# A two-block transformer kernel on Trainium2: other instruction orders in four feed-forward layers and in the head of the latent attention

## The reference, cut to what matters

```python
# first_block, D_MODEL 1024, SEQ 512, DEPTH 2, D_FF 2816
sc = silu(c)
for i in range(2):
    mod = (sc @ ada_w[i] + ada_b[i]).reshape(B, 9, 1024)        # shifts, scales, gates
    x = modulated_sublayer(x, mod[:, 0:3], ..., swiglu)          # ffn0, then ffn2
    x = modulated_sublayer(x, mod[:, 3:6], ..., pool_mixer if i == 0 else mla_mixer)
    x = modulated_sublayer(x, mod[:, 6:9], ..., swiglu)          # ffn1, then ffn3
# swiglu: (silu(gate) * up) @ w_out, gate and up = split(h @ w_in)
# mla_mixer, 16 heads:
lat = h @ w_in; c_q, c_kv, k_r = split(lat, [256, 384])
c_q = rmsnorm(c_q, q_norm); c_kv = rmsnorm(c_kv, kv_norm)
q = einsum(c_q, w_uq); q_rope = apply_rope(q[..., 64:], cos, sin) * ATTN_SCALE
k_rope = apply_rope(k_r, cos, sin); q_lat = einsum(q[..., :64], w_uk) * ATTN_SCALE
p = softmax(q_lat . c_kv + q_rope . k_rope); o = ((p . c_kv) . w_uv) @ w_o
# second_block: two hybrid layers of stick-breaking and sparse attention (the change does not touch them)
```

## Time and profile before

| | us |
|---|---|
| median of 3 runs | 2932.2 |
| lowest and highest | 2930.58, 2932.82 |
| the profiled execution | 2932.32 |
| its span | 2930.5 |
| TensorE busy | 2805.9 |
| mean granted clock of TensorE | 0.984 |

### The profile page before, as it was taken

How to read it: one execution, slowest core, us unless ns; L and a number is a source line. 1 busy time by engine, 2 the same in 40 slices (tenths; PEclk the granted TensorE clock), 3 DMA queues, 4 the chain that set the end, 5 groups by cost and what they waited for, 6 DMA issues and landing times. The chain is left out here.

```text
span 2930.5 us, 42964 instructions
## 1 busy us (share of the span) xinstructions
PE 2805.9 (96%) x16774; PEld 2451.4 (84%) x16774; DVE 2185.0 (75%) x3427; ACT 1448.7 (49%) x2390; POOL 401.0 (14%) x297
## 2 busy tenths in 40 slices
PE   8999989999999999799999999999899999999999
PEld 7998778998889988677799988787788778877887
DVE  7888778888778877899687755387677663866773
ACT  6555235555255542566465632464555435555552
POOL 0010111000101001100300000404300233141003
PEclk9999999999999999999999999999999999999999
DMA  7675733665636656200245432402211232022113
GB/s 271 194 224 172 238 126 76 207 203 174 233 115 214 208 168 215 73 12 19 101 119 162 145 107 87 136 15 83 91 52 58 96 127 72 30 94 72 54 56 115
DMA packets 103065, 367.40 MB, mean 125 GB/s; under 512 B 11984, under 2 KB 14800, under 8 KB 102352
## 3 DMA queue, kind: packets, MB, share of 16 engines
q1 hardware_dynamic: 73968, 262.95, 25.8%
q0 software_dynamic: 26304, 90.19, 11.7%
q10 hardware_dynamic: 2592, 11.51, 1.1%
HBM read 354.12 MB, written 6.29 MB: 123 GB/s over the span
## 5 line engine op out<-in xcount | busy, mean ns | idle before, releaser
L464 ACT ACTIVATE w_hi<-raw 128x1024 fp32r<-128x1024 f32 x351 | 366.8, 1053 | 320.1 <-DMA raw<-stream_in 179.1
L485 POOL TENSOR_TENSOR w_lo<-raw,w_hi 128x1024 fp32r<-128x1024 f32 x109 | 274.2, 2522 | 1265.1 <-ACT w_hi L464 1265.0
L506 PE MATMUL psum<-h_hi,w_hi 128*128 128x256 f32 (+1 forms) x1609 | 352.3, 329 | 8.5 <-DVE h_lo L699 3.4
L506 PE MATMUL psum<-h_lo,w_hi 128*128 128x256 f32 (+1 forms) x1609 | 345.4, 325 | 0.0
L506 PE MATMUL psum<-h_hi,w_lo 128*128 128x256 f32 (+1 forms) x1609 | 345.2, 325 | 0.0
L479 DVE TENSOR_TENSOR w_lo<-raw,w_hi 128x1024 fp32r<-128x1024 f32 x202 | 247.2, 1227 | 83.1 <-ACT w_hi L464 82.9
L506 PE MATMUL psum<-t_hi,w_hi 128*128 128x256 f32 (+1 forms) x1536 | 284.9, 300 | 19.9 <-ACT sq L1156 7.5
L464 ACT ACTIVATE w_hi<-xr 128x1024 fp32r<-128x1024 f32 x202 | 213.5, 1057 | 160.6 <-DVE xr L1271 68.6
L506 PEld LDWEIGHTS psum<-h_hi,w_hi 128*128 128x128 f32 x1609 | 251.0, 188 | 44.1 <-DVE w_lo L479 5.8
L506 PE MATMUL psum<-t_hi,w_lo 128*128 128x256 f32 (+1 forms) x1536 | 283.3, 299 | 0.0
L506 PEld LDWEIGHTS psum<-h_lo,w_hi 128*128 128x128 f32 x1609 | 252.0, 188 | 26.9
(11 more groups left out here) (527 smaller groups left out, 5568.4 us busy)
## 6 DMA issues: line engine op xcount, KB each, us to landing
raw<-stream_in SPq DMA_DIRECT2D x351, 512.0 KB, 3.4
ada_raw<-ada_in POOLq DMA_DIRECT2D x128, 512.0 KB, 5.3
xr<-stream_in SPq DMA_DIRECT2D x122, 512.0 KB, 4.6
xr<-stream_in POOLq DMA_DIRECT2D x40, 512.0 KB, 5.5
ada_in_t<-ada_in SPq DMA_DIRECT2D x8, 512.0 KB, 12.0
x_held<-X ACTq DMA_DIRECT2D x2, 2048.0 KB, 6.8
X<-x_held ACTq DMA_DIRECT2D x2, 2048.0 KB, 7.9
X<-xT_in SPq DMA_DIRECT2D x4, 512.0 KB, 5.5
```

The costliest lines, as they stand in the source:

```text
L464: act.activation(w_hi[:, u % RING], tile, ACT.Copy, scale=-1.0 if u in negated else 1.0).then_inc(hi_ready, 1)
L485: pool.tensor_tensor(w_lo[:, u % RING], source[u][0], w_hi[:, u % RING].bitcast(F32), ALU.subtract).then_inc(lo_ready, 1)
L506: mm = pe.matmul(dst, w[wi], m[mi], start=(first and n == 0), stop=(last and n == total - 1), skip_group_check=skip)
```

## The change

In the feed-forward layers a table `PAIR_ROWS` gives each pair its own number of rows. ffn0 gets 22 rows in its pairs (two in pairs 1 and 2, three in pairs 3 to 8; the third stands behind the second weight sum of the next pair) and 26 in its down stage; ffn1 and ffn2 keep two rows in each of pairs 1 to 8 and get another order of their 24 rows in the down stage, with none behind the second unit. GpSimd's queue issues as many transfers per pair as the pair has rows, still ahead of the accumulating transfer. In pair 0 of all four layers the copy of the third product stands ahead of the sixth unit's high half and of the high half of a sum.

In the latent attention ScalarE copies and scales the rotary banks (before, VectorE did), VectorE multiplies by the cosine straight from PSUM into `lat`, the low halves of the first query unit, the keys and the values are made by VectorE, and those of the rotary unit and from the second query unit on by GpSimd as before. ScalarE makes the second query unit's high half after the four rotary high halves.

```diff
@@ -290,7 +290,7 @@
         snap = Signal(sem("products_kept"))
         joined = Signal(sem("products_joined"))
         parts_negated, odd_added = sem("parts_negated"), sem("odd_added")
-        t2_copied = sem("t2_copied")
+        t2_copied, rotary_copied = sem("t2_copied"), sem("rotary_copied")
         a_hi_ready = Signal(sem("a_hi_ready"))
         a_ready = Signal(sem("a_ready"))
 
@@ -1005,10 +1005,11 @@
 
         ADA = {"ffn0": range(2, 8), "ffn1": range(8, 13), "ffn2": range(13, 18), "ffn3": ()}
         SHIFT_BY_PE = (1, 2, 4, 6)
-        FIRST_PAIR = {"ffn0": 1, "ffn1": 1, "ffn2": 1}
+        PAIR_ROWS = {"ffn0": (0, 2, 2, 3, 3, 3, 3, 3, 3, 0), "ffn1": (0,) + 8 * (2,) + (0,),
+                     "ffn2": (0,) + 8 * (2,) + (0,)}
         FIRST_ROWS = {"ffn0": 0, "ffn1": 0, "ffn2": 0}
-        DOWN_ROWS = {"ffn0": (0, 1, 1, 2, 2, 1, 2, 2, 1, 2, 2, 1, 2, 2, 1, 2, 2, 1, 2, 2, 1, 0, 0, 0),
-                     "ffn1": (0, 1, 1, 1, 1, 1, 1, 2, 1, 1, 2, 1, 1, 2, 1, 1, 1, 2, 1, 1, 1, 0, 0, 0)}
+        DOWN_ROWS = {"ffn0": (0, 0, 1, 2, 1, 1, 2, 1, 1, 2, 1, 1, 2, 1, 1, 2, 1, 1, 2, 2, 1, 0, 0, 0),
+                     "ffn1": (0, 0, 1, 1, 2, 1, 1, 2, 1, 1, 2, 1, 1, 2, 1, 1, 2, 1, 1, 1, 1, 0, 0, 0)}
         DOWN_ROWS["ffn2"] = DOWN_ROWS["ffn1"]
 
 
@@ -1019,13 +1020,13 @@
 
         def ada_pair_dve(dve, L, j, m):
 
-            if ADA[L] and FIRST_PAIR[L] <= j < PAIRS - 1:
-                ada_blocks_dve(dve, L, FIRST_ROWS[L] + 2 * (j - FIRST_PAIR[L]) + m, 1)
+            if ADA[L] and m < PAIR_ROWS[L][j]:
+                ada_blocks_dve(dve, L, FIRST_ROWS[L] + sum(PAIR_ROWS[L][:j]) + m, 1)
 
         def ada_down_dve(dve, L, k):
 
             if ADA[L]:
-                ada_blocks_dve(dve, L, FIRST_ROWS[L] + 2 * (PAIRS - 1 - FIRST_PAIR[L]) + sum(DOWN_ROWS[L][:k]), DOWN_ROWS[L][k])
+                ada_blocks_dve(dve, L, FIRST_ROWS[L] + sum(PAIR_ROWS[L]) + sum(DOWN_ROWS[L][:k]), DOWN_ROWS[L][k])
 
         def pair_banks(j):
 
@@ -1186,12 +1187,15 @@
             if final:
                 a_hi_act(act, L, 0)
             keep_act(act, L, j, "p5", 1, "v2")
+            if j == 0:
+                keep_act(act, L, j, "u2", 2, "g2")
             split_hi(act, u + 5)
             if final:
                 a_hi_act(act, L, 1)
             if j == 0:
                 combine_hi_act(act, L, T4)
-            keep_act(act, L, j, "u2", 2, "g2")
+            else:
+                keep_act(act, L, j, "u2", 2, "g2")
             split_hi(act, u + 6)
             if final:
                 a_hi_act(act, L, 2)
@@ -1323,6 +1327,7 @@
                 a_lo_dve(dve, L, 3)
             split_lo(dve, u + 8)
             sum_2_dve(dve, L, j + 1)
+            ada_pair_dve(dve, L, j, 2)
             up_sum_dve(dve, L, j)
             if final:
                 a_lo_dve(dve, L, 4)
@@ -1433,10 +1438,9 @@
                     ada_piece(pool, t)
                     t += 1
             for j in range(PAIRS):
-                if ADA[L] and FIRST_PAIR[L] <= j < PAIRS - 1:
+                for _ in range(PAIR_ROWS[L][j] if ADA[L] else 0):
                     ada_piece(pool, t)
-                    ada_piece(pool, t + 1)
-                    t += 2
+                    t += 1
                 add_weights(pool, L, j + 1)
             if ADA[L]:
                 for t in range(t, min((ADA[L][-1] + 1) * NC + 2, 18 * NC)):
@@ -2004,7 +2008,7 @@
                 prod.give(mm, ("u", u) if c == 3 else ("g", g + c))
             first_products = mla_extra(L)
             for r in range(4):
-                pe.wait_ge(evac.sem, evac.at(("g", g + r)))
+                pe.wait_ge(rotary_copied, r + 1)
                 if r:
                     pe.wait_ge(scaled.sem, scaled.at((L, "rot", r - 2 if r >= 2 else "k")))
                 sums.give(pe.matmul(psum[:, ROTARY_BANKS[r % 2]], mconst[:], rotary(r), start=True, stop=True),
@@ -2065,17 +2069,29 @@
             for c in range(2):
                 split_value_act(act, (L, "cq", c), ta[:, c], cq_hi[:, c])
             split_value_act(act, (L, "kv"), tb[:, 0], kv_hi[:])
+            u, g = u + 4, g + 4
+
+            def copy_rotary(r):
+
+                act.wait_ge(prod.sem, prod.at(("g", g + r)))
+                act.activation(rotary(r), bank(g + r), ACT.Copy, scale=ATTN_SCALE).then_inc(rotary_copied, 1)
+            split_hi(act, u + 1)
+            act.wait_ge(h_ready.sem, h_ready.at((L, "cq", 1)))
+            copy_rotary(0)
+            split_hi(act, u + 2)
+            copy_rotary(1)
             act.wait_ge(scaled.sem, scaled.at((L, "rot", "k")))
             for rows, first in ((slice(64, 96), 0), (slice(32, 64), 1)):
                 op = act.activation(kt_hi[rows, first:4:2], tb[rows, 1:2].broadcast_to((32, 2, S)), ACT.Copy)
             part_hi.give(op, (L, "rot", "k"))
-            u, g = u + 4, g + 4
-            for k in range(1, 5):
-                split_hi(act, u + k)
+            copy_rotary(2)
+            copy_rotary(3)
+            split_hi(act, u + 3)
             for r in range(4):
                 if r == 2:
                     mla_extra(L)(act, "act", -1)
-                split_value_act(act, (L, "rot", r), tb[:, r % 2], qr_hi[:, r])
+                split_value_act(act, (L, "rot", r), lat[:, r], qr_hi[:, r])
+            split_hi(act, u + 4)
             softmax_act(act, L, mla_attention, mla_extra(L))
             u, g = own[L, "wo"], own[L, "wog"]
             split_hi(act, u + 1)
@@ -2119,36 +2135,43 @@
             split_value_dve(dve, (L, "kv"), tb[:, 0], kv_hi[:], kv_lo[:])
             dve.wait_ge(stage_loaded, own[L, "loaded"])
             rotate_dve(dve, order, (L, "rot", "k"), lat[:, 3], mrope[:, 0], mrope[:, 1], psum[:, 4], tb[:, 1])
+            u, g = u + 4, g + 4
+
+            def by_cosine(r):
+                dve.wait_ge(rotary_copied, r + 1)
+                evac.give(dve.scalar_tensor_tensor(out=lat[:, r], in0=bank(g + r), scalar=ATTN_SCALE, in1=mrope[:, 0],
+                                                   op0=ALU.mult, op1=ALU.mult), ("g", g + r))
+
+            def by_sine(r):
+                dve.wait_ge(sums.sem, sums.at((L, "rot", r)))
+                order.step(dve.tensor_tensor((std, rstd)[r % 2][:], psum[:, ROTARY_BANKS[r % 2]], mrope[:, 1],
+                                             ALU.mult))
+                dve.wait_ge(evac.sem, evac.at(("g", g + r)))
+                scaled.give(dve.tensor_tensor(lat[:, r], lat[:, r], (std, rstd)[r % 2][:], ALU.add),
+                            (L, "rot", r))
+            dve.wait_ge(lo_ready, u + 1)
+            split_lo(dve, u + 1, early=True)
+            by_cosine(0)
+            by_cosine(1)
+            split_lo(dve, u + 2, early=True)
+            by_cosine(2)
+            by_cosine(3)
+            by_sine(0)
+            by_sine(1)
             dve.wait_ge(part_hi.sem, part_hi.at((L, "rot", "k")))
             for rows, first in ((slice(64, 96), 0), (slice(32, 64), 1)):
                 op = dve.tensor_tensor(kt_lo[rows, first:4:2], tb[rows, 1:2].broadcast_to((32, 2, S)),
                                        kt_hi[rows, first:4:2].bitcast(F32), ALU.subtract)
             h_ready.give(op, (L, "rot", "k"))
-            u, g = u + 4, g + 4
-            for r in range(4):
-                dve.wait_ge(prod.sem, prod.at(("g", g + r)))
-                evac.give(dve.tensor_scalar(rotary(r), bank(g + r), ATTN_SCALE, None, ALU.mult), ("g", g + r))
-            def by_cosine(r):
-                dve.wait_ge(evac.sem, evac.at(("g", g + r)))
-                dve.wait_ge(h_ready.sem, h_ready.at((L, "rot", r - 2 if r >= 2 else "k")))
-                order.link(dve.tensor_tensor(tb[:, r % 2], rotary(r), mrope[:, 0], ALU.mult))
-
-            def by_sine(r):
-                dve.wait_ge(sums.sem, sums.at((L, "rot", r)))
-                order.step(dve.tensor_tensor((std, rstd)[r % 2][:], psum[:, ROTARY_BANKS[r % 2]], mrope[:, 1],
-                                             ALU.mult))
-                scaled.give(dve.tensor_tensor(tb[:, r % 2], tb[:, r % 2], (std, rstd)[r % 2][:], ALU.add),
-                            (L, "rot", r))
-            for first in (0, 2):
-                by_cosine(first)
-                by_cosine(first + 1)
-                by_sine(first)
-                by_sine(first + 1)
-                if first == 2:
-                    dve.wait_ge(part_hi.sem, part_hi.at((L, "zeros")))
-                    mla_extra(L)(dve, "dve", -1)
-                for r in (first, first + 1):
-                    split_value_dve(dve, (L, "rot", r), tb[:, r % 2], qr_hi[:, r], qr_lo[:, r])
+            split_lo(dve, u + 3, early=True)
+            for r in (0, 1):
+                split_value_dve(dve, (L, "rot", r), lat[:, r], qr_hi[:, r], qr_lo[:, r])
+            dve.wait_ge(part_hi.sem, part_hi.at((L, "zeros")))
+            mla_extra(L)(dve, "dve", -1)
+            by_sine(2)
+            by_sine(3)
+            for r in (2, 3):
```

(4 more changed lines are left out.)

## The result

The changed kernel takes 2947.4 us in the median of four runs (2946.1 to 2948.3), the kernel before in four runs beside it 2931.4: the ratio is 1.0054, with a 95% interval from 1.0039 to 1.0070. It is slower by half a per cent, and the interval leaves out 1. The prediction said 2949.4 us, slower. The changed kernel's profiled execution has a span of 2944.9 us, 14.4 more than that of before.

The account below looks back on a forecast made before the run. TensorE was taken to bound the kernel, busy 96% of the span, with VectorE ending the pairs. Terms 27.7 - 5.6 - 3.6 - 0.8 - 3.6 + 3.0 = +17.1 us on 2932.3 gave 2949.4 us, range 2937 to 2958.

Parts of the forecast that it names:

- the row that leaves the second unit: Down stages of three layers: one row (1.22 us) moves from ahead of the last activation low half; -1.2 us each.
- first layer, pairs: Pairs 3 to 8: third row delays the accumulating transfer on GpSimd's queue, period 24.5 us over 19.89; +27.7 us (18.1 to 31.9).
- first layer, down stage: 26 rows instead of 32 end three TensorE waits for weights, -5.6 us; one row leaving the second unit, -1.2 us.
- second layer: One row leaves the down stage's second unit, -1.2 us; earlier copy of the third product in the first pair, -0.8 us.
- third layer: One row leaves the down stage's second unit, -1.2 us; the first pair's earlier copy gains zero.
- latent attention: Head of the attention: scores start later because the rotary rows' transfers wait on SyncE's queue; +3.0 us.
- last layer: First pair, no rows: earlier third-product copy ends TensorE's 1.9 us wait and the half clock's 1.7; -3.6 us.
- the bound above: First layer's pairs: upper bound of 7.6 us for the accumulating transfer's landing, from the third of three transfers.
- Rival 4: First layer's six pairs: half clock after TensorE's waits makes it last in the pair, 10.2 us more, 2959.6 us; chance 0.08.
- SyncE's wait: Attention's head: rotary transfers issue only after a fetch whose buffer GpSimd's second-query-unit low half frees; scores 3.0 us later.
- First pairs: Pair 0, four layers: earlier third-product copy ends TensorE's 1.9 us wait; kept 0.8 us in second, 3.6 in last layer.
- Rival 1: Pairs and attention: neither queue holds anything, pairs cost 7.3 us and the attention wins 5.2; 2920.8 us, chance 0.08.

Follow-up runs that it names:

- the rows alone: Kernel before with only the first layer's row changes: its tables, the third row in pairs 3 to 8 and `ffn_pool`; 2952.4 us, ratio 1.0069.
- the old rows: Changed kernel with the first layer's rows as before the change (two in pairs 1 to 8, 32 in its down stage); 2931.8 us, ratio 0.9991.
- the order of two transfers: Changed kernel with the accumulating transfer issued ahead of the third row's transfer in the six three-row pairs; 2924.1 us, ratio 0.9971.
- the version with both moves: Changed kernel, accumulating transfer ahead of the third row's and second query unit's high half ahead of the rotary high halves; 2916.7 us, ratio 0.9952.
- the kernel with the high half moved: Changed kernel with ScalarE making the second query unit's high half before the four rotary high halves; 2939.6 us, ratio 1.0023.

## Why the prediction was right, and where a size was off

Set side by side, instruction by instruction of TensorE, the two first profiles give each step's share (the rows "first layer, down stage", "second layer" and "third layer" hold the prediction's -1.2 us for the row that leaves the second unit):

| step | predicted us | measured us |
|---|---|---|
| first layer, pairs | +27.7 | +31.9 |
| first layer, down stage | -6.8 | -9.3 |
| second layer | -2.0 | -2.0 |
| third layer | -1.2 | -1.3 |
| latent attention | +3.0 | +4.2 |
| last layer | -3.6 | -3.7 |
| what no step covers, first block | 0 | -2.1 |
| second block | 0 | -3.3 |
| sum | +17.1 | +14.4 |

The total is nearer than its terms, and that is luck: pairs and attention cost 5.4 us more than forecast, and the down stage and the two lines without a step took 7.9 back. Those two lines are scatter as far as the runs show it: 3.3 us of the second block (above), and most of the 2.1 is TensorE at a clock of 0.50 at the ends of the second layer and of the attention, for 10.3 and 3.4 us in the first profile of before, for 6.9 us and not at all in that of the changed kernel; over all thirteen profiles the first stretch lasts 3.4 to 10.3 us and the second up to 6.9.

**Pairs.** The mechanism is shown by three runs: the rows alone bring the loss, the old rows undo most of it, and the order of two transfers takes back all but VectorE's 1.22 us a row. The size was 4 us short. The period was 25.0 to 25.5 us instead of 24.5, for the landing that no row of before showed took 7.4 us, not the 6.9 that I took from the second of three transfers; 7.6, the bound above, was closer; and VectorE's stretch took 14.61 us in the pair shown, not 14.40. Issued without a row's transfer right ahead, the same transfer landed in 5.9. The Trainium skill (DMA: Bandwidth & Descriptors, Anatomy of one DMA) would have 3.2 us, as an estimate, for either; both rows disagree.

**Rival 4, the clock**, was right about half of it. TensorE fell to half clock at each of the six waits, yet VectorE's mark at the end of the pairs moved by 32.0 us (254.58 to 286.53), as TensorE's did: the half clock lay under VectorE's loop, which the prediction gave as the reason against it.

**Down stage.** The three waits went as said; some 2.5 us more went with them, 1.0 of it a wait for ScalarE at the layer's end, which the prediction didn't have. The row that leaves the second unit did what was forecast: TensorE's wait there falls from 1.49 to 0.34 us in the first and second layer and from 1.49 to 0.33 in the third. Only the traces show it; no run takes it by itself.

**Attention.** SyncE's wait was there, and moving one instruction removes it. Of the 1.2 us that were missing, the landing of the fourth rotary transfer took 2.5 us instead of 2.0, and the last rotary sum ended 0.4 us later than worked out. GpSimd's start was named rightly. What the prediction left out is TensorE's 4.84 us wait for the low half of the values' unit. It lies inside the longer chain and cost at most those 0.4 us: the last rotary products come behind it, and VectorE's order of time has a short pause for them:

```profile
1254.96 0.69 DVE L2147 TENSOR_TENSOR rstd<-psum,mrope 128x512 f32<-128x512 f32 x1 [0.29 <-PE psum L2014]
```

**First pairs.** Three layers keep 0.8 us or less of TensorE's 1.9 us and the last keeps it all, as predicted; the half clock behind it follows in some executions and not in others, so its 1.7 us are a chance, not a constant.

**Rival 1** is the version with both moves: neither queue holds anything. It was priced at 2920.8 us, 0.9961 of the kernel before, and measured at 0.9952. That is near in part by luck: the attention won 3.2 us (23.8 instead of 27.0 from the first query product to the scores), not 5.2, since GpSimd's low half now runs beside VectorE's two rotary lows and makes them some 2.1 us longer; the down stage's further 2.5 us made up for it.

## What to carry to other kernels

Where an engine issues transfers in order, a transfer added for one purpose holds whatever is queued behind it until its own wait is over: read the queue's order before you count the new work, and put the transfer that someone waits for ahead of the one that must wait. When a step is moved, follow what it frees (here a buffer, then a fetch, then the transfers behind that fetch), for the wait turns up two engines away. And removing a wait pays only up to the next one in the chain: moving the low half of the values' unit, and the copies in three layers, gave TensorE its time back, and it waited nearly as long later on.

## What the runs showed of the hardware that was not expected

**A GpSimd instruction beside VectorE.** An instruction of VectorE with two operands in SBUF took three times as long while GpSimd's low half ran, and ended just after it. Orders of time of GpSimd and of VectorE, the version with the low half of the values' unit moved:

```profile
1219.84 2.56 POOL L485 TENSOR_TENSOR w_lo<-raw,w_hi 128x1024 fp32r<-128x1024 f32 x1 [13.21 <-ACT w_hi L464]
```

```profile
1220.10 0.68 DVE L2151 TENSOR_TENSOR rstd<-psum,mrope 128x512 f32<-128x512 f32 x1
1220.82 2.13 DVE L2154 TENSOR_TENSOR lat<-lat,rstd 128x512 f32<-128x512 f32 x1
1222.97 2.44 DVE L2168 TENSOR_TENSOR kt_lo<-tb,kt_hi 32x1024 fp32r<-32x1024 f32 x2
```

The first of VectorE's rows reads PSUM and one SBUF operand and takes its usual 0.68 us; the second has two in SBUF and takes 2.13 instead of 0.69, ending 0.55 us after GpSimd's (1222.40); the key low halves, which took 4.5 us beside GpSimd, take 2.44 alone. In the kernel with the high half moved the same befell a rotary low (3.44 us for two, above). The Trainium skill (SBUF — State Buffer, SBUF: two separate sides) says that where VectorE's instruction has two SBUF inputs and GpSimd's reads SBUF, the one which starts first keeps a shared pair of ports for its whole instruction and the other is blocked; these rows agree.

**TensorE's pace at one granted clock.** Eight pairs of the last layer took 128.0 us of TensorE's time in twelve of thirteen profiles and 123.2 in one, the second profile of the kernel before. The same windows (columns as in the earlier trace rows) of the kernel before and of its repetition:

```profile
1549.44:1677.46 128.02, 128.02 (x1089) 128.02 (x1088) 99.14 (x100) 71.73 (x89) 5.18 (x6) 1.00 0.51 157
```

```profile
1551.55:1674.74 123.19, 123.19 (x1089) 123.19 (x1088) 98.18 (x100) 70.68 (x88) 5.17 (x6) 1.00 0.53 164
```

Same instructions, no wait, a granted clock of 1.00 in both, 3.8% apart. No run here shows a cause. It is 4.8 us in one stage, a third of what this change moved, so a difference of that size between two single profiles proves nothing by itself.
